# Half-head swap for the rotary embedding: on-chip DMA into two buffers in place of a permutation product on TensorE

## What is computed

```python
def _rope(x, cos, sin):
    half = HEAD_DIM // 2
    x1, x2 = x[..., :half], x[..., half:]
    return jnp.concatenate([x1 * cos - x2 * sin, x2 * cos + x1 * sin], axis=-1)
...
    z = u @ w_in
    q, k, v, p, g_a, g_p = jnp.split(z, [i1, i2, i3, i4, i5], axis=-1)
    q = _rope(_rmsnorm(q.reshape(B, S, N_HEADS, HEAD_DIM), q_norm_g), cos, sin)
    k = _rope(_rmsnorm(k.reshape(B, S, N_KV_HEADS, HEAD_DIM), k_norm_g), cos, sin)
    y_attn = _window_attention(q, k, v, sinks) @ w_attn_o
    y_pool = _multiscale_pool(p, w_pool_grp, pool_scale) @ w_pool_o
    merged = jax.nn.sigmoid(g_a) * y_attn + jax.nn.sigmoid(g_p) * y_pool
```

## Time and profile before

| | |
|---|---|
| median of 3 runs | 2077.24 us (2074.61 to 2077.28) |
| profiled execution, its own time | 2076.52 us |
| span of the profiled execution | 2074.7 us |
| granted TensorE clock, mean | 0.997 |
| TensorE matmuls in flight | 98% of the span |
| TensorE's share of the chain that ended last | 95% |
| VectorE, ScalarE, GpSimd busy | 46%, 27%, 32% |

### The profile page before, as it was taken

The page is one execution under the profiler, slowest core; times in us unless marked ns, Lnnn a source line. Parts: engine busy times, 40 slices in busy tenths (PEclk is TensorE's granted clock), DMA queues, the critical chain, the costliest instruction groups (busy, mean ns, idle before and its releaser), DMA issues.

```text
span 2074.7 us, 24433 instructions
## 1 busy us (share of the span) xinstructions
PE 2038.8 (98%) x10117; PEld 1700.4 (82%) x10117; DVE 953.7 (46%) x1389; ACT 553.7 (27%) x808; POOL 673.8 (32%) x274
## 2 busy tenths in 40 slices
PE   5999999999999999999999999999999999999999
PEld 4788888897888987888898888889878888888888
DVE  5654255366546755211256533445555666221121
ACT  2222122233422422122232211223243233221220
POOL 0345435502000245443434542452100004543451
PEclk9999999999999999999999999999999999999999
DMA  9465366522224366333326654652221435332331
GB/s 274 132 203 183 112 182 199 132 72 69 73 68 130 91 204 188 118 98 109 126 70 177 203 157 125 200 184 66 72 82 61 120 124 142 100 104 82 101 106 67
DMA packets 329066, 264.78 MB, mean 128 GB/s; under 512 B 24878, under 2 KB 310910, under 8 KB 328958
## 3 DMA queue, kind: packets, MB, share of 16 engines
q1 hardware_dynamic: 327296, 262.70, 42.6%
q10 hardware_dynamic: 1662, 0.54, 0.1%
HBM read 261.11 MB, written 2.10 MB: 127 GB/s over the span
## 4 chain that ended last, share of the span: by engine, by line
PE 95%; DVE 3%; DMA 1%; issue 1%; ACT 0%; POOL 0%; ACTq 0%; DVEq 0%
PE bank L1328 27%; PE bank L1330 27%; PE bank L1329 27%; PE bank L1404 1%; PE bank L1408 1%; PE bank L1405 1%; PE bank L1355 1%; PE bank L1357 1%; PE bank L1356 1%; PE ps L1537 1%; PE ps L1519 1%; DMA stage<-in_w_out 1%; PE ps L1495 0%; PE bank L1638 0%; PE ps L1502 0%
## 5 line engine op out<-in xcount | busy, mean ns | idle before, releaser
L588 POOL TENSOR_TENSOR w_lo<-stage,w_hi 128x1024 fp32r<-128x1024 f32 (+1 forms) x237 | 647.3, 2751 | 1210.3 <-ACT w_hi L639 1171.1
L1328 PE MATMUL bank<-u_hi,w_hi 128*128 128x512 f32 x1768 | 698.7, 395 | 3.7 <-POOL w_lo L588 3.5
L1330 PE MATMUL bank<-u_hi,w_lo 128*128 128x512 f32 x1768 | 689.3, 390 | 0.0
L1329 PE MATMUL bank<-u_lo,w_hi 128*128 128x512 f32 x1768 | 688.7, 390 | 0.0
L639 ACT ACTIVATE w_hi<-stage 128x1024 fp32r<-128x1024 f32 (+2 forms) x336 | 349.5, 1074 | 585.6 <-DMA stage<-in_w_ff_up 334.5
L1328 PEld LDWEIGHTS bank<-u_hi,w_hi 128*128 128x128 f32 x1768 | 332.4, 188 | 78.7 <-issue 10.8
L1329 PEld LDWEIGHTS bank<-u_lo,w_hi 128*128 128x128 f32 x1768 | 332.5, 188 | 69.6 <-issue 2.4
L1330 PEld LDWEIGHTS bank<-u_hi,w_lo 128*128 128x128 f32 x1768 | 332.2, 188 | 70.0
L1003 DVE TENSOR_TENSOR prod<-silu,bank 128x512 f32<-128x512 f32 x88 | 60.5, 688 | 522.3 <-PE bank L1330 503.9
L1328 PE MATMUL bank<-h_hi,w_hi 128*128 128x512 f32 x744 | 290.2, 390 | 1.0 <-DVE h_lo L1008 1.0
L1330 PE MATMUL bank<-h_hi,w_lo 128*128 128x512 f32 x744 | 289.5, 389 | 0.0
(11 more groups left out here) (176 smaller groups left out, 1488.2 us busy)
## 6 DMA issues: line engine op xcount, KB each, us to landing
stage<-in_w_ff_up SPq DMA_DIRECT2D x176, 512.0 KB
ada_stage<-in_w_ada SPq DMA_DIRECT2D x128, 512.0 KB, 4.8
stage<-in_w_ff_down SPq DMA_DIRECT2D x32, 1408.0 KB
stage<-in_w_in SPq DMA_DIRECT2D x18, 1024.0 KB
ada_block<-in_w_ada SPq DMA_DIRECT2D x8, 1024.0 KB, 12.1
stage<-in_w_out SPq DMA_DIRECT2D x8, 1024.0 KB
stage<-in_w_in SPq DMA_DIRECT2D x16, 256.0 KB
stage<-in_w_in SPq DMA_DIRECT2D x8, 512.0 KB
```

The source lines that it names most:

```text
L588: nc.gpsimd.tensor_tensor(stage_tile(w_lo, kind, n), t, hi_tile(n, depth(kind, n)), ALU.subtract).then_inc(lo_ready, 1)
L1328: mm(bank[n % BANKS][:, :], hi[:, k, :], rhs_hi(k), start=(k == 0), stop=False)
L1329: mm(bank[n % BANKS][:, :], hi[:, k, :], rhs_lo(k), start=False, stop=False)
L1330: last = mm(bank[n % BANKS][:, :], lo[:, k, :], rhs_hi(k), start=False, stop=(k == k_n - 1))
```

## The change

The permutation matrix leaves the constants (a row of them goes from 324 to 196 numbers), and `swap_qk` leaves TensorE. ScalarE's queue gets `swap_halves(l, i)` at the head of the pool part of step 6 + i, i = 0 to 4: it waits for the normalisation of i, and for i >= 2 until rope i - 2 has read the buffer, and issues four DMAs of 32 partitions x 2 KB, from `qk_raw` to one of two buffers `qk_turn` in the second and third row of `r_g`. VectorE's rope waits for the DMA semaphore of its buffer and reads the swapped values from SBUF, where it read ps7. Since the buffers lie where `gate_a` 1 and 2 are written, ScalarE's gate tanh waits for the last rope from gate tile 1 on, where it did from 3 on. On VectorE `pool_out(2)` in step 10 moves ahead of `rope(4)`.

```diff
-K_ID, K_SWAP, K_HEADS, K_FREQ, K_SIGN, K_CNT = 0, P, 2 * P, 2 * P + 2, 2 * P + 3, 2 * P + 4
+K_ID, K_HEADS, K_FREQ, K_SIGN, K_CNT = 0, P, P + 2, P + 3, P + 4
...
+        qk_turn = [at(f"qk_turn{b}", [P, S], F32, r_g + (1 + b) * KB2) for b in range(2)]
...
-        qk_swapped = sem("qk_swapped")
+        qk_swapped = [sem(f"qk_swapped{b}") for b in range(2)]
...
+            def swap_halves(l, i):
+
+                act.wait_ge(qk_normed, l * 5 + i + 1)
+                if i >= 2:
+                    act.wait_ge(rope_step, l * 15 + 3 * (i - 2) + 2)
+                for q in range(4):
+                    half = HEAD // 2
+                    act.dma_start(qk_turn[i % 2][q * half:(q + 1) * half, :],
+                                  qk_raw[(q ^ 1) * half:((q ^ 1) + 1) * half, QK[i], :]).then_inc(qk_swapped[i % 2], 16)
...
+                    if T_P <= n <= T_P + 4:
+                        swap_halves(l, n - T_P)
...
-                        if 3 <= g < KT:
+                        if 1 <= g < KT:
                             act.wait_ge(rope_step, l * 15 + 15)
...
-                dve.wait_ge(qk_swapped, l * 5 + i + 1)
+                dve.wait_ge(qk_swapped[i % 2], 64 * (l * (3, 2)[i % 2] + i // 2 + 1))
...
-                nc.vector.tensor_tensor(rope_b[:, :], ps7[:, :], sin_t[:, :], ALU.mult).then_inc(rope_step, 1)
+                nc.vector.tensor_tensor(rope_b[:, :], qk_turn[i % 2][:, :], sin_t[:, :], ALU.mult).then_inc(rope_step, 1)
...
+                    if T_P + 2 <= n <= T_P + 5:
+                        pool_out(l, n - T_P - 2)
                     if n == T_P + 4:
                         rope(l, 4)
-                    if T_P + 2 <= n <= T_P + 5:
-                        pool_out(l, n - T_P - 2)
...
-            def swap_qk(l, i):
-                pe.wait_ge(qk_normed, l * 5 + i + 1)
-                if i:
-                    pe.wait_ge(rope_step, l * 15 + 3 * i - 1)
-                mm(ps7[:, :], swap, qk_raw[:, QK[i], :], start=True, stop=True).then_inc(qk_swapped, 1)
...
-                            swap_qk(l, n - T_P - 1)
                             spread_qk(l, n - T_P)
...
-                    if n == T_P + 4:
-                        swap_qk(l, 4)
```

More of the change, by code:

```diff
@@ L150, in shape_constants @@
     k[row, K_ID + row] = 1.0
-    k[row, K_SWAP + (row // HEAD) * HEAD + (row % HEAD + HEAD // 2) % HEAD] = 1.0
     k[row, K_HEADS + row // HEAD] = 1.0
@@ L267, in trunk @@
         ident = consts_s[:, K_ID:K_ID + P]
-        swap = consts_s[:, K_SWAP:K_SWAP + P]
         heads = consts_s[:, K_HEADS:K_HEADS + 2]
```

## The result

The median went from 2077.26 us (2074.61 to 2078.24, four runs) to **2105.55 us** (2105.28 to 2107.04, four runs): the ratio is 1.0137, with an interval of 1.0124 to 1.015. That is 28.3 us slower, where 6.3 were forecast (2083.5, and 2092 at the most). The profiled execution took 2105.28 us, its span is 2103.4 us, 28.7 longer than before.

The account below looks back on a forecast made before the run. TensorE was taken as the bound (98% of the span), with VectorE right behind it in the mixing stretch. 6.0 of net waits + 0.6 for rope_b - 0.3 for constants = +6.3, so 2083.5 us; range 2077.5 to 2092.

Parts of the forecast that it names:

- what is taken away: Ten permutation products leave TensorE, five a layer, 0.86 us each: 4.3 us a layer, 8.6 in all.
- the ring: Token mixing: normalisation, issues, pool copy, scale, rounding, low_part, pool_mix, rope, back to normalisation; 8.75 us a turn, TensorE's 7.27.
- the landing: Last of a tile's four copies lands 2.2 us after its issue; hidden for tiles 1 to 3.
- What is added to ScalarE: Four DMA issues for each of five tiles a layer, 0.40 us each, 1.6 for the four.
- Two small terms: rope_b with two SBUF operands: 0.1 us a turn, 0.6 in all, at most 3.3; narrower constants gain 0.3.
- The walk: Layer 0, tile by tile: TensorE waits 0.4, 1.4, 1.4 and 4.0 us before the pool groups; 3.0 slower a layer.
- late landing: Rival: copies queue behind weight loads, landing in 4.6 us or more; 7.8 slower a layer, 2093; 0.15 together with dear issues.
- All of it reaches the end: Behind the mixing stretch TensorE has no idle time to make up a delay, so the whole 6.0 us counts.
- The rival that was to apply the rule in full: Rival: rope_b waits for whole GpSimd window additions, 2.4 us more, 2086; counted within the forecast's 0.55.
- The hidden swap: Rival: ScalarE's issues under 0.1 us each, ring turns in 7.15, only the tail waits; 7 us gained, 2070; chance 0.10.
- the low prices: Rival: same ring, issues 0.365 us apart, landing 2.0; +4.1 us, between 2076 and 2081; chance 0.20.
- The dear issues: Rival: ScalarE's issues cost 0.66 us each; 8.7 slower a layer, 2094; 0.15 together with late landing.

Follow-up runs that it names:

- experiment 1: Kernel before with the permutation products left out and nothing in their place, so the swap isn't computed: 2068.75 us, ratio 0.9958.
- experiment 2: Changed kernel with one straight DMA of 128 partitions a tile in place of four, halves not swapped: 2087.06 us, ratio 1.0048.
- experiment 3: Changed kernel with the sine table copied by ScalarE into PSUM once a layer, so rope_b reads one operand from there: 2097.16 us, ratio 1.0095.
- experiment 5: Changed kernel with the same four DMAs issued from SyncE's queue between the weight loads, not ScalarE's: 2089.39 us, ratio 1.0054.
- experiment 6: Changed kernel with VectorE's normalisation of the next tile and the spreading of its scale ahead of the rope in steps 7 to 10: 2080.28 us.
- experiment 10: Changed kernel with 8, 8, 10 and 23 extra unused matmuls ahead of the four pool groups of each layer: 2104.3 us, ratio 1.0125.

## Why the direction was right and the size wrong

**Right: what is taken away.** 8.6 were forecast for the ten products; experiment 1 gives 8.5, with an interval of 5.6 to 11.8. Its two stretches give 3.7 + 4.6 = 8.2; that the rest agrees so closely is luck, as opening, middle and end moved by +1.4, -2.9 and +1.2.

**Right: the ring.** The chain shows its members in the forecast order, TensorE waits at the named matmul four times a layer, and the way was settled by shortening single members or putting them elsewhere (experiments 2, 3, 5 and 6).

**Right: the landing.** 2.0 in the median against 2.2, hidden for tiles 1 to 3. In the changed kernel it is hidden for the first and the last swap too, where the prediction looked for a wait of VectorE, since other members are later. The window sums of group 3 and the gate tanh cost nothing, as said.

**Wrong: the sizes of what stands in the ring.** The step that failed is "What is added to ScalarE", which put the four issues at 1.6, together with the port term of "Two small terms", which put the rope's delay at 0.1 a turn. They measured 2.54 and 1.44. The walk also left out one wait and the clock. Layer 0 piece by piece, forecast and measured:

- Each turn, 8.75 and 10.99. The block of issues took 2.54, not 1.6 (0.94 more). It is 0.64 an issue, where 0.40 was taken from two plain loads at the kernel's start; the row of the sinks, 0.66, was the nearer one and had been kept only as a bound. The rope took 3.5, not 2.06 (1.44 more), where 0.1 had been taken from L1049's median. The other members are within 0.05 of their rows, and handing over took about 0.1 less.
- From normalisation 0 to 1, 6.94 and 8.95: 2.0 more. Here the walk left something out. It costed the landing as the way to rope 0, but low_part of step 6 stands on VectorE ahead of rope 0 and waits for a rounding that now stands behind the block of issues (476.46, after 3.92 of idling for ScalarE). The landing itself was no wait. From this place comes the wait in mid-tile as well, before the spreading products (L1506, 6.3 in five waits): they need the norms that VectorE widens behind each normalisation. The prediction held such a wait for a sign that only a late landing gives; here it came with a landing of 2.0.
- From normalisation 1 to 2, 8.1 and 10.4: the same two sizes, 2.3.
- Two turns, to normalisation 4: 2 x 2.25 = 4.5.
- From there to the fourth pool group, 8.34 and 8.84: 0.5. The last of the four issues begins 0.7 later behind the normalisation than forecast (1.86 and 1.2), and rope 4 and what stands around it took 0.2 less.
- From the fourth pool group to row_max, 7.5 (508.02 to 515.50) and 9.25: 1.8. That is the clock, which stands at 0.50 behind a wait of 6.0. A forecast wait of 4.0 should have raised the question (in layer 1 the wait was 4.4, and the clock fell too); no row of before has such a wait in this stretch.

2.0 + 2.3 + 4.5 + 0.5 + 1.8 = 11.1, and with the forecast 3.0 that is 14.1, against 14.0 measured. Layer 1 took 15.2 by the same places; the clock alone is 2.8 there. "All of it reaches the end" held to within the 2.8 by which the part behind the stretch of layer 0 got shorter (experiment 10).

**The port.** On the bare rows, L1049's maximum of 1.24 set the upper bound of 3.3 in all; experiment 3 measures 8.4, beyond it. The bound took one instruction a rope, and took its longest record for the longest possible. That record was itself such a meeting, with what was left of a GpSimd addition in rope 4 of layer 1. The other L1049 say nothing of rope_b: in rope 1 to 3 they begin just ahead of the addition (481.01 and 481.19 in the kernel before). What the bound missed is that rope 1 to 3 stand right behind pool_mix, whose end starts GpSimd's additions, so that the next operation meets one each time (rope_b takes 1.53 in these six and 0.68 in the other four). The Trainium skill's page "SBUF — State Buffer", section "Who interferes with whom", says just that of an operation with two SBUF inputs beside a GpSimd operation that reads SBUF: whoever comes second waits for the whole of the first. The trace agrees: both end 0.55 behind the addition that they met. The rival that was to apply the rule in full (2.4 more) counted too little even so. Its 3 us are 0.5 a rope, but three additions take 3.85, so six whole ones are 7.7; and it had no second meeting.

**The rivals.** The hidden swap needed issues under 0.2 and the low prices issues 0.365 apart; both fail on 0.64. The late landing fails on 2.0. The dear issues, "8.7 a layer, 2094", had the right price for the issues and the rope's old price: experiment 3, which is that case, took 2097.16. So the issue price explains the way from 2083.5 to about 2095, and the rope 8.4 of the rest. The constants' 0.3 was nothing. What isn't settled is the 0.5 to 1.3 by which the end, behind the last row_max, is longer in most kernels without the product.

## What to carry to other kernels

A transfer that lands in the shadow isn't free: its issue occupies the engine whose queue it is on, and whatever that engine does next is late by the whole block. Before putting small DMAs on an engine, follow the order behind them until it comes back to where it started; in a ring every price counts once a turn, and moving one member out of it (the rope behind the normalisation) was worth 25 us where the work itself was unchanged. Put the DMAs on a queue whose engine has nothing urgent behind them, and price the neighbours of each moved operand: here GpSimd was started by VectorE's own pool_mix, and the second operation behind that, once it read two SBUF operands, met GpSimd every time.

## What the runs showed of the hardware

- Four DMA issues in a row on one engine, each 32 partitions by 2 KB from SBUF to SBUF, took 0.51 for the first (0.62 in one block) and 0.61 for the others, 2.54 until the engine's next instruction; one of 128 partitions with the same total bytes took 0.49. So between these two the number of issues made the price, not the bytes. Single issues took up to 1.9 in other orders.
- Such a copy of 64 KB landed in 1.9 to 3.1 us from its issue, median 2.0; in the orders with the normalisation first the median was 3.0 to 3.3 and the maximum 5.5.
- A 128x512 VectorE operation with two SBUF operands took 1.53 in place of 0.68 beside a GpSimd addition, and pushed the next one, 0.81, to 1.41; with one of the first one's operands in PSUM they were 0.68 and 0.81.
- After a wait of 6.0 us TensorE's granted clock was 0.50 until some 3.5 us into its new work, which cost 1.7 to 1.8 us; after one of 4.4 in layer 1 it was 0.50 too, which cost 2.8. Behind the six waits of 2.3 to 3.3 it fell to 0.50 twice and stayed at 1.00 four times. With the waits filled it stayed at 1.00 in these places.
